# Three mixers: the last output product runs its last three weight units, not two, one half of the tokens at a time

## The chip, the cores and the metric

The kernel runs on one core of one Trainium2 chip. The metric is the device time of one execution in microseconds (us). TensorE (PE) multiplies matrices into PSUM, VectorE (DVE), ScalarE (ACT) and GpSimd (POOL) do the rest, SyncE (SP) issues the weight loads. Each engine takes its own list of instructions in order and waits on counters (semaphores) that the others raise.

## The reference, cut to what matters

Two blocks run over 256 tokens of width 1024, in eight sublayers in all, numbered s = 0 to 7. Sublayers 0, 3 and 6 are the three mixers (sparse attention with a convolution, differential attention, a gated recurrence); the others are SwiGLUs. Each mixer ends in a product of its 256x1024 result with a 1024x1024 output weight, and then a gated residual and a norm lead to the next sublayer's input:

```
# s = 0
mixed = jnp.concatenate([attn, conv_out], axis=-1)
mix = mixed @ w_out
x = layer_norm(DEEPNORM_ALPHA * x + g1[:, None, :] * mix, ln1_g[l], ln1_b[l])
ff = swiglu(modulate(x, sh2, sc2), w_gate[l], w_up[l], w_down[l])
...
# s = 3 and s = 6
y = diff_attention(...)      # ends in   o.reshape(B, S, H * dv) @ w_o
y = hgrn2(...)               # ends in   o.reshape(B, S, D_MODEL) @ w_o
x = x + gate[:, :, 1] * y
h = rms_norm(x, norm_g[layer, 2]) * (1.0 + scale[:, :, 2]) + shift[:, :, 2]
x = x + 0.5 * gate[:, :, 2] * swiglu_2(h, ffn_w_in[layer, 1], ffn_w_down[layer, 1])
```

## The kernel before

**Weights.** All large weights stream through a ring of three slots, in units of 128x2048 numbers (1 MB). SP loads a unit into `raw`; ACT copies its high part to `whi` (function `hi`, line 534), DVE takes the rest to `wlo` (function `lo`, line 910), and PE multiplies. A product of full precision is three matmuls: high times high, high times rest, rest times high (`three`, line 1523). A unit has a number; `w_used` counts the units that PE is done with, and `hi(unit)` waits until PE is done with the unit three places earlier, whose slot it takes. ACT executes whatever comes behind that `hi` only afterwards.

**Tokens.** The 256 tokens are two halves t = 0, 1 of 128. The output weight of a mixer is four units, here called u0 to u3. `rows_of` multiplies one unit with one token half: two halves h of the 1024 output columns, two slices of the contraction, three matmuls each, 12 matmuls of 512 columns. `down_rows` does that for both token halves of a unit and raises `w_used`. The sum over the four units grows in PSUM, banks 0 and 1 for t = 0, banks 2 and 3 for t = 1.

**The end of a sublayer.** `close` does the last two units by token half: t = 0 of both, then t = 1 of both. So the result of t = 0 is complete while PE still has work on t = 1. Between them PE does `sum_columns` (line 1633, 32 records: the next sublayer's shift and scale columns) and `transpose_inputs(s + 1, 0)` (line 1622, eight transposes of the new t = 0 input). For s = 0 both come after all four pieces.

**What answers to it on the other engines**, for s = 3 and 6. DVE (`conclude`): the residual of t = 0 (lines 966 and 971, halves h), `lo` of the next sublayer's first unit F (F takes the slot of u1), the new columns (lines 932, 937), `modulate` of t = 0 (line 944), the residual of t = 1 with the rest parts of the new input (line 952). ACT: `hi` of u3, `hi(F)`, then `leave`: two squares of t = 0 (line 565), the scaled copy of t = 0 (line 572) once POOL has taken the root (lines 462, 465), `modulate` (line 541), high parts (line 546), the first square of t = 1, `hi(F + 1)`, the second square, the scaled copy of t = 1. For s = 0 there are no squares on ACT: DVE sums the moments itself (lines 966, 977, 978), and the layer norm follows (lines 987, 989).

**The next sublayer** starts with `enter`: 12 matmuls of t = 0, the eight transposes of t = 1, and so on. In s = 0 DVE also adds up pieces of a large weight for the shift and scale columns (line 925), which arrive by DMA.

The order of each engine's list is written out by hand; nothing reorders it.

Of the kernel before, what the change touches and what calls it, by code (L numbers as in the profile page):

```python
# [30 lines left out]
P = 128  # L31
# [10 lines left out]
NSUB = 8  # L42
# [40 lines left out]
LATE_GATES = (1, 4, 7)  # L83
# [61 lines left out]
def two_blocks(  # L145
# [29 lines left out]
    with ExitStack() as ctx:  # L175
# [15 lines left out]
        hhi = sb("hhi", [P, KT, TOK], F32R)  # L191
        hlo = sb("hlo", [P, KT, TOK], F32R)
# [48 lines left out]
        def bank(b, n=1):  # L241
            return psf[:, b * BANK:(b + n) * BANK]
# [3 lines left out]
        w_hi, w_lo, w_used = sem("w_hi"), sem("w_lo"), sem("w_used")  # L246
# [7 lines left out]
        y_ready, x_new, root = sem("y_ready"), sem("x_new"), sem("root")  # L254
# [1263 lines left out]
        def _(pe):  # L1518
# [57 lines left out]
                                     g == 0 and k == 0 and ct % 2 == 0, g == 1 and k == 3, weights_move=False)  # L1576
                done.then_inc(w_used, 1)

            def rows_of(unit, hi_of, lo_of, t, first, final, lap=0, signal=None):

                slot = unit % RING
                if t == 0:
                    pe.wait_ge(w_lo, unit + 1 + RING * lap)
                for h in range(2):
                    for k in range(2):
                        cols = slice(k * D + h * BANK, k * D + (h + 1) * BANK)
                        done = three(bank(2 * t + h), hi_of(k, t), lo_of(k, t), whi[:, slot, cols], wlo[:, slot, cols],
                                     first and k == 0, final and k == 1)
                    if signal and h == 0:
                        done.then_inc(signal, 1)  # L1590
                return done

            def down_rows(unit, hi_of, lo_of, first, lap=0, before=None):

                for t in range(NT):
                    if before:
                        before(t)
                    done = rows_of(unit, hi_of, lo_of, t, first, False, lap)
                done.then_inc(w_used, 1)

            def close(s, one, two, before_one, before_two):

                before_one(0)
                rows_of(*one, 0, False, False)
                before_two()
                rows_of(*two, 0, False, True, signal=y_ready).then_inc(y_ready, 1)
                if 0 < s < NSUB - 1:
                    sum_columns(s + 1)
                before_one(1)
                rows_of(*one, 1, False, False).then_inc(w_used, 1)  # L1610
                if 1 < s < NSUB - 1:
                    transpose_inputs(s + 1, 0)
                rows_of(*two, 1, False, True, signal=y_ready).then_inc(w_used, 1)
                if s == 0:
                    sum_columns(1)
                if s < 2:
                    transpose_inputs(s + 1, 0)
# [19 lines left out]
            def sum_gate(s):  # L1637

                pe.wait_ge(a_used, pieces_until(s, 2) if s else KT)
                for h in range(2):  # L1640
                    done = pe.matmul(bank(gate_bank(s) + h), ones[:, :], ada_acc[:, s % 2, 2 * D + h * BANK:2 * D + (h + 1) * BANK],
                                     start=True, stop=True)
                done.then_inc(gate_sum, 1)

            def transpose_inputs(s, t):

                src = xs if s < 2 else xn
                for g in range(2):
                    if s == 0:
                        pe.wait_ge(x_land, 32)  # L1650
                        pe.wait_ge(vec_set, 1)
                    elif s == 1:
                        pe.wait_ge(x_new, 2 * t + g + 1)
                    else:
                        pe.wait_ge(h_src, 4 * (s - 2) + 2 * t + g + 1)
                    transposes([src[:, t, (4 * g + k) * P:(4 * g + k + 1) * P] for k in range(4)], 2 * t + g, h_tr)

            def output_product(s, unit, mixed_ready, k0=0):

                def place(j):  # L1660
                    k_j = (k0 + 2 * j) % KT
                    return (unit + j, lambda k, t: hhi[:, k_j + k, t * P:(t + 1) * P],
                            lambda k, t: hlo[:, k_j + k, t * P:(t + 1) * P])

                def mixed(j, t):
                    if (j, t) in mixed_ready:
                        pe.wait_ge(mix_lo, mixed_ready[j, t])

                for j in range(2):
                    down_rows(*place(j), j == 0, before=lambda t: mixed(j, t))  # L1670
                close(s, place(2), place(3), lambda t: mixed(2, t), lambda: None)

            def swiglu(s):
                m, turned = SWIGLUS.index(s) * NCH, SWIGLUS.index(s) * (NCH + 1)
                U = FIRST[s]

                def gate_up(unit, g, i, lap=0):

                    for t in range(NT):
                        if g == 0:  # L1680
                            pe.wait_ge(act_ready, 2 * (m + i) - 1 + t)
                        done = columns_of(unit, g, t, 4 + t, lap=lap)
                        if g == 1 and t == 0:
                            done.then_inc(gu_ready, 1)
                    done.then_inc(w_used, 1)

                def turn(i):
                    pe.wait_ge(act_ready, 2 * (m + i + 1))
                    pe.wait_ge(alo_ready, turned + i)
                    for k in range(2):  # L1690
                        for t in range(NT):
                            done = pe.transpose(ps[:, 6, k * TOK + t * P:k * TOK + (t + 1) * P],  # L1692
                                                act[:, t, k * P:(k + 1) * P], ident)
                    done.then_inc(tr_ready, 1)

                def last_turn(t):
                    pe.wait_ge(act_ready, 2 * (m + NCH - 1) + t + 1)
                    pe.wait_ge(alo_ready, turned + NCH - 1 + t)
                    for k in range(2):
                        done = pe.transpose(ps[:, 6, k * TOK + t * P:k * TOK + (t + 1) * P],  # L1700
                                            act[:, t, k * P:(k + 1) * P], ident)
                    done.then_inc(tr_ready, 1)

                def kept(unit):
                    return unit, lambda k, t: ahi[:, k, t * P:(t + 1) * P], lambda k, t: alo[:, k, t * P:(t + 1) * P]

                def body(first, i, lap=0, first_down=False):
                    gate_up(first, 0, i, lap)
                    if first_down and s not in LATE_GATES:
                        pe.wait_ge(gate_set, s + 1)  # L1710
                    turn(i - 1)
                    gate_up(first + 1, 1, i, lap)
                    pe.wait_ge(alo_ready, turned + i)
                    down_rows(*kept(first + 2), first_down, lap=lap)

                enter(s, (4, 5), gu_ready)
                body(U + 2, 1, first_down=True)
                if s == 1:

                    pe.wait_ge(toe_fill, 2)  # L1720
                    pe.wait_ge(cols_set, 2)
                    for h in range(HEADS):
                        if h >= 2:
                            pe.wait_ge(toe_rows, h - 1)
                        pe.matmul(ps[:, 6 + h % 2, 0:TOE], big[0:BUCKETS + 1, 2560 + h * P:2560 + (h + 1) * P],
                                  big[0:BUCKETS + 1, 2048:2048 + TOE], start=True, stop=True).then_inc(toe_mm, 1)
                    pe.wait_ge(toe_rows, HEADS)
                with pe.Fori(2, NCH - 1) as i:
                    body(U + 5, i, i - 2)
                last = U + 3 * (NCH - 1) - 1  # L1730
                gate_up(last, 0, NCH - 1)
                turn(NCH - 2)
                gate_up(last + 1, 1, NCH - 1)
                last_turn(0)

                def before_last():
                    last_turn(1)
                    if s in LATE_GATES:
                        sum_gate(s)

                def before_last_but_one(t):
                    if t == 1:
                        pe.wait_ge(alo_ready, turned + NCH + 1)

                close(s, kept(last + 2), (last + 3, lambda k, t: hhi[:, k, t * P:(t + 1) * P],
                                          lambda k, t: hlo[:, k, t * P:(t + 1) * P]), before_last_but_one, before_last)

            def attention():

# [286 lines left out]
```

## Time and profile before

| | |
|---|---|
| median of 3 runs | 1611.03 us (1610.11 to 1612.12) |
| the profiled execution's own time | 1611.54 us |
| its span, first to last instruction | 1609.5 us |
| PE busy | 1439.1 us, 89% |
| DVE, ACT, POOL busy | 68%, 42%, 12% |
| mean granted TensorE clock | 0.927 of 2.4 GHz |
| chain that ended last, on PE | 72% |

The profile counts an engine as busy while its compute instructions run. In a row of the timeline, the bracket at the end is how long the engine stood idle before and which instruction released it. The chain of waits is followed back from the last instruction, so its pieces show what each moment of the time was spent on. PEclk is the granted TensorE clock: 1.00 is 2.4 GHz and 0.50 is 1.2 GHz.

### The profile page before, as it was taken

The page shows a single profiled execution, that of the slowest core. Times are in us where ns is not written, and L with a number is a line of the kernel's source. Part 1 is how long each engine was busy: PE and PEld are TensorE (multiplying, and loading weights), DVE is VectorE, ACT ScalarE, POOL GpSimd, SP SyncE. Part 2 cuts the span into 40 slices and gives each one's busy share as a digit, 9 for nine tenths or more (in the row PEclk, how much of TensorE's full clock was granted, in tenths as well). Part 3 has the DMA queues.
Part 4 walks back from the last instruction along what each step waited for, and adds up shares of the span by engine and source line. Part 5 has one row for each costly group of instructions (what it writes and reads, how often), then busy time and mean ns, then how long its engine had stood idle before and what let it go on. Part 6 is the DMA issues. An engine that isn't in the chain of part 4 may idle for free.

```text
span 1609.5 us, 19253 instructions
## 1 busy us (share of the span) xinstructions
PE 1439.1 (89%) x6855; PEld 1193.9 (74%) x6855; DVE 1095.0 (68%) x1103; ACT 673.6 (42%) x788; POOL 193.8 (12%) x271
## 2 busy tenths in 40 slices
PE   1786769999889999996899999999999896899999
PEld 1785557888668888773678888788888785778887
DVE  4678674777657886657557775688865796455554
ACT  0433124444343443545364434544446752254432
POOL 1101230111031110210011110211101000100000
PEclk9887769999989999996799999999999997799999
DMA  7751726999558996450168895699944440146662
GB/s 298 255 184 29 247 73 204 311 317 325 179 195 290 352 335 211 147 193 0 54 220 297 306 312 168 221 320 337 348 157 158 154 134 26 53 152 220 210 224 80
DMA packets 183812, 333.97 MB, mean 208 GB/s; under 512 B 8666, under 2 KB 122943, under 8 KB 182610
## 3 DMA queue, kind: packets, MB, share of 16 engines
q1 hardware_dynamic: 157328, 237.95, 44.0%
q0 software_dynamic: 26112, 95.07, 16.6%
q8 instruction: 33, 0.54, 0.1%
q10 hardware_dynamic: 322, 0.27, 0.1%
q14 instruction: 17, 0.14, 0.0%
HBM read 330.64 MB, written 2.62 MB: 207 GB/s over the span
## 4 chain that ended last, share of the span: by engine, by line
PE 72%; DVE 15%; ACT 5%; DMA 3%; issue 2%; POOL 2%; ACTq 0%; POOLq 0%; DVEq 0%
PE ps L1523 65%; DVE wlo L910 2%; DMA ada_raw<-in_w_ada 2%; PE ps L1633 2%; PE ps L1622 1%; PE ps L1692 1%; DVE ada_acc L1464 1%; ACT whi L534 1%; ACT hf L541 1%; DMA raw<-in_w_ada 1%; DVE xn L966 1%; DVE ada_acc L925 1%; POOL st L462 1%; DVE ada_acc L1084 1%; DVE hlo L952 1%
## 5 line engine op out<-in xcount | busy, mean ns | idle before, releaser
L910 DVE TENSOR_TENSOR wlo<-raw,whi 128x2048 fp32r<-128x2048 f32 x215 | 490.4, 2285 | 164.7 <-ACT whi L534 164.3
L1523 PE MATMUL ps<-whi,hhi 128*128 128x512 f32 (+1 forms) x1208 | 490.2, 406 | 36.6 <-DVE hlo L952 16.0
L534 ACT ACTIVATE whi<-raw 128x2048 fp32r<-128x2048 f32 x215 | 410.0, 1910 | 244.4 <-PE ps L1523 217.7
L1523 PE MATMUL ps<-wlo,hhi 128*128 128x512 f32 (+1 forms) x1208 | 479.4, 397 | 0.0
L1523 PE MATMUL ps<-whi,hlo 128*128 128x512 f32 (+1 forms) x1208 | 479.1, 397 | 0.0
L1523 PEld LDWEIGHTS ps<-whi,hhi 128*128 128x128 f32 x1208 | 232.7, 193 | 92.9 <-DVE wlo L910 18.1
L1523 PEld LDWEIGHTS ps<-whi,hlo 128*128 128x128 f32 x1208 | 232.3, 192 | 50.3
L1523 PEld LDWEIGHTS ps<-wlo,hhi 128*128 128x128 f32 x1208 | 233.0, 193 | 46.5 <-issue 0.7
L925 DVE SCALAR_TENSOR_TENSOR ada_acc<-ada_raw,csil,ada_acc 128x1024 f32<-128x1024 f32 x120 | 150.3, 1278 | 13.1 <-DMA ada_raw<-in_w_ada 11.1
L1523 PE MATMUL ps<-whi,ahi 128*128 128x512 f32 x400 | 158.6, 396 | 0.0
L1523 PE MATMUL ps<-whi,alo 128*128 128x512 f32 x400 | 157.6, 394 | 0.0
L1523 PE MATMUL ps<-wlo,ahi 128*128 128x512 f32 x400 | 157.6, 394 | 0.0
L441 POOL DMA_DIRECT2D ada_raw<-in_ada_w x96 | 50.9, 530 | 542.4 <-DVE ada_acc L925 538.4
L610 ACT ACTIVATE ahi<-ps 128x512 fp32r<-128x512 f32 x50 | 29.9, 599 | 189.9 <-PE ps L1692 189.9
L606 ACT ACTIVATE act<-ps 128x256 f32<-128x256 f32 x110 | 42.2, 384 | 152.7 <-PE ps L1523 152.7
L1040 DVE TENSOR_TENSOR alo<-ps,ahi 128x512 fp32r<-128x512 f32 x50 | 34.5, 691 | 94.4 <-ACT ahi L610 94.4
L1523 PEld LDWEIGHTS ps<-whi,alo 128*128 128x128 f32 x400 | 76.2, 191 | 16.2
L1523 PEld LDWEIGHTS ps<-wlo,ahi 128*128 128x128 f32 x400 | 76.3, 191 | 15.8
L1523 PEld LDWEIGHTS ps<-whi,ahi 128*128 128x128 f32 x400 | 76.4, 191 | 15.7
L1523 PE MATMUL ps<-hhi,whi 128*128 128x256 f32 x224 | 67.1, 300 | 11.7 <-DVE wlo L910 11.7
L1523 PE MATMUL ps<-hhi,wlo 128*128 128x256 f32 x224 | 66.2, 296 | 0.0
L1523 PE MATMUL ps<-hlo,whi 128*128 128x256 f32 x224 | 66.0, 295 | 0.0
(237 smaller groups left out, 1389.9 us busy)
## 6 DMA issues: line engine op xcount, KB each, us to landing
raw<-in_ffn_w_in SPq DMA_DIRECT2D x176, 512.0 KB
ada_raw<-in_ada_w POOLq DMA_DIRECT2D x96, 512.0 KB, 5.2
raw<-in_ffn_w_down SPq DMA_DIRECT2D x44, 1024.0 KB
big<-in_ada_w POOLq DMA_DIRECT2D x48, 512.0 KB, 6.1
ada_raw<-in_w_ada POOLq DMA_DIRECT2D x32, 512.0 KB, 4.8
raw<-in_hgrn_w_in SPq DMA_DIRECT2D x16, 1024.0 KB
raw<-in_attn_w_qkv SPq DMA_DIRECT2D x12, 1024.0 KB
raw<-in_w_gate SPq DMA_DIRECT2D x22, 512.0 KB
```

Source lines behind the costliest of these rows:

```text
L441: pool.dma_start(ada_slot(p), w[bass.ds(kt * P, P), first + j * D:first + (j + 1) * D])\
L462: pool.tensor_scalar(mean, mean, st[:, 251 + 2 * t:252 + 2 * t], EPS2, ALU.add, ALU.add).then_inc(root_in, 1)
L534: sc.activation(whi[:, slot, 0:n], raw[:, slot, 0:n], ACT.Copy).then_inc(w_hi, 1)
L541: done = sc.activation(hf[:, kt, t * P:(t + 1) * P], ps[:, 2 * t + 1, k * P:(k + 1) * P], ACT.Identity, scale=modc[:, s % 2, 8 + kt:9 + kt ...
L606: sc.activation(act[:, t, :], ps[:, 4 + t, 0:FC], ACT.Silu).then_inc(silu_done, 1)
L610: sc.activation(ahi.rearrange("p k n -> p (k n)"), bank(6), ACT.Copy).then_inc(ahi_ready, 1)
L910: ve.tensor_tensor(wlo[:, slot, 0:n], raw[:, slot, 0:n], whi[:, slot, 0:n].bitcast(F32), ALU.subtract)\
L925: ve.scalar_tensor_tensor(acc, ada_slot(p), csil[:, bass.ds((0 if a < 2 else 8) + kt, 1)], acc, ALU.mult, ALU.add).then_inc(a_used, 1)
L952: ve.tensor_tensor(hlo[part], hf[part], hhi[part].bitcast(F32), ALU.subtract).then_inc(h_lo, 1)
L1040: ve.tensor_tensor(a_lo, bank(6), a_hi.bitcast(F32), ALU.subtract).then_inc(alo_ready, 1)
L1523: done = pe.matmul(dst, lhsT, rhs, start=first and n == 0, stop=final and n == 2, skip_group_check=True)
L1633: done = pe.matmul(ps[:, COL_BANK, j:j + 1], ada_acc[:, s % 2, j * P:(j + 1) * P], ones[:, 0:1], start=True, stop=True)
```

## The change

`close` takes a list of units in place of two. For the mixers the list has three, u1 to u3, and only u0 is done by `down_rows`; for the SwiGLUs it still has two, in the order as before. With three units the eight transposes of the next input stand between the two column halves (h = 0 and h = 1) of the last unit at t = 1, not ahead of that unit.

```
-            def rows_of(unit, hi_of, lo_of, t, first, final, lap=0, signal=None):
+            def rows_of(unit, hi_of, lo_of, t, first, final, lap=0, signal=None, between=None):
...
+                    if between and h == 0:
+                        between()
...
-            def close(s, one, two, before_one, before_two):
+            def close(s, places, before):
 
-                before_one(0)
-                rows_of(*one, 0, False, False)
-                before_two()
-                rows_of(*two, 0, False, True, signal=y_ready).then_inc(y_ready, 1)
+                last = len(places) - 1
+                for j, place in enumerate(places):
+                    before(j, 0)
+                    done = rows_of(*place, 0, False, j == last, signal=y_ready if j == last else None)
+                done.then_inc(y_ready, 1)
                 if 0 < s < NSUB - 1:
                     sum_columns(s + 1)
-                before_one(1)
-                rows_of(*one, 1, False, False).then_inc(w_used, 1)
-                if 1 < s < NSUB - 1:
-                    transpose_inputs(s + 1, 0)
-                rows_of(*two, 1, False, True, signal=y_ready).then_inc(w_used, 1)
+                for j, place in enumerate(places):
+                    turning = (lambda: transpose_inputs(s + 1, 0)) if j == last and 1 < s < NSUB - 1 else None
+                    if turning and last == 1:
+                        turning()
+                    before(j, 1)
+                    rows_of(*place, 1, False, j == last, signal=y_ready if j == last else None,
+                            between=turning if last > 1 else None).then_inc(w_used, 1)
...
-                for j in range(2):
-                    down_rows(*place(j), j == 0, before=lambda t: mixed(j, t))
-                close(s, place(2), place(3), lambda t: mixed(2, t), lambda: None)
+                down_rows(*place(0), True, before=lambda t: mixed(0, t))
+                close(s, [place(j) for j in range(1, 4)], lambda j, t: mixed(j + 1, t))
```

The first place is PE's list at the end of sublayer 3, from the matmuls on t = 0 to those on t = 1. A row that waits for `mix_lo` is the first matmul of u2 on a token half. Before, u2 at t = 0 comes behind all of u1, and after `sum_columns` (the rows on `ada_acc`) u2 follows at once:

```order
L1523 MATMUL ps<-whi,hhi 128x512 [waits w_lo,mix_lo]
L1523 MATMUL ps<-wlo,hhi 128x512
...
L1633 MATMUL ps<-ones,ada_acc 128x1 [waits cols_set,a_used]
L1633 MATMUL ps<-ones,ada_acc 128x1 x15
L1523 MATMUL ps<-whi,hhi 128x512 [waits mix_lo]
L1523 MATMUL ps<-wlo,hhi 128x512
```

Now:

```order
L1638 MATMUL ps<-ones,ada_acc 128x1 [waits cols_set,a_used]
L1638 MATMUL ps<-ones,ada_acc 128x1 x15
L1523 MATMUL ps<-whi,hhi 128x512
L1523 MATMUL ps<-wlo,hhi 128x512
L1523 MATMUL ps<-whi,hlo 128x512
...
L1523 MATMUL ps<-whi,hhi 128x512 [waits mix_lo]
```

The 12 matmuls of u1 on t = 1 moved from ahead of u2 and u3 at t = 0 to behind `sum_columns`. `w_used` for u1 is raised by the last of them, so its place moved too.

The second place is PE's list a little later: the eight transposes of sublayer 4's first token half (the rows on `xn`) and what follows them. Before, 12 matmuls of u3 lie behind them, of which the last three are shown, ahead of the first matmul of sublayer 4 (the row that waits for `h_lo`):

```order
L1622 MATMUL ps<-kc,xn 128x128 [waits h_src]
L1622 MATMUL ps<-kc,xn 128x128 x3
...
L1523 MATMUL ps<-whi,hhi 128x512
L1523 MATMUL ps<-wlo,hhi 128x512
L1523 MATMUL ps<-whi,hlo 128x512
L1523 MATMUL ps<-whi,hhi 128x512 [waits h_lo,w_lo]
```

Now six matmuls lie between, all shown:

```order
L1627 MATMUL ps<-kc,xn 128x128 [waits h_src]
L1627 MATMUL ps<-kc,xn 128x128 x3
L1523 MATMUL ps<-whi,hhi 128x512
L1523 MATMUL ps<-wlo,hhi 128x512
L1523 MATMUL ps<-whi,hlo 128x512
L1523 MATMUL ps<-whi,hhi 128x512
L1523 MATMUL ps<-wlo,hhi 128x512
L1523 MATMUL ps<-whi,hlo 128x512
L1523 MATMUL ps<-whi,hhi 128x512 [waits h_lo,w_lo]
```

The transposes moved behind six more matmuls. The lists of ACT, DVE, POOL and SP are the same before and after. ACT's at this place, where the three rows on `whi` are `hi` of u2, u3 and F:

```order
L534 ACTIVATE whi<-raw 128x2048 [waits w_used,w_land0]
L534 ACTIVATE whi<-raw 128x2048 [waits w_used,w_land1]
L534 ACTIVATE whi<-raw 128x2048 [waits w_used,w_land2]
L565 ACTIVATE xn,st<-xs 128x512 [waits x_new] x2
L572 ACTIVATE xn<-xs,st 128x512 [waits root]
```

Nothing moved there; the two squares and the scaled copy stand behind the `hi` of F, as before.

## Rows read from the trace of the kernel before

**Rows 1.** The page, busy time (share of the span) xinstructions.
```profile
PE 1439.1 (89%) x6855; PEld 1193.9 (74%) x6855; DVE 1095.0 (68%) x1103; ACT 673.6 (42%) x788; POOL 193.8 (12%) x271
```

**Rows 2.** What TensorE waited for, 776 to 832 us: us, times, longest.
```profile
PE ps L1622 <- DVE big L1353: 4.8, 1, 4.8
PE ps L1622 <- ACT xn L572: 2.8, 1, 2.8
PE ps L1523 <- DVE hlo L952: 0.8, 1, 0.8
```

**Rows 3.** Chain of waits, end of sublayer 3: start us, us, what.
```profile
799.46 3.47 PE ps L1633 x32
802.93 2.89 PE ps L1523 x12
...
806.69 1.40 PE ps L1523 x6
```

**Rows 4.** Timeline of ACT, end of sublayer 3: start us, us.
```profile
794.12 1.92 ACT L534 ACTIVATE whi<-raw 128x2048 fp32r<-128x2048 f32 x1 [3.52 <-PE ps L1523]
799.66 0.63 ACT L565 ACTIVATE xn<-xs 128x512 f32<-128x512 f32 x1 [3.63 <-DVE xs L971]
...
800.99 0.63 ACT L565 ACTIVATE xn<-xs 128x512 f32<-128x512 f32 x1 [0.60 <-DVE xs L971]
...
804.01 1.34 ACT L572 ACTIVATE xn<-xs,st 128x512 f32<-128x512 f32 x2 [2.29 <-POOL st L465]
806.79 1.50 ACT L541 ACTIVATE hf<-ps,modc 128x128 f32<-128x128 f32 x4 [1.44 <-PE ps L1622]
...
810.19 1.90 ACT L534 ACTIVATE whi<-raw 128x2048 fp32r<-128x2048 f32 x1
812.00 0.61 ACT L565 ACTIVATE xn<-xs 128x512 f32<-128x512 f32 x1
```

**Rows 5.** Timeline of DVE, the same stretch.
```profile
798.21 0.69 DVE L966 TENSOR_TENSOR xn<-ps,gate 128x512 f32<-128x512 f32 x1 [5.29 <-PE ps L1523]
...
800.87 2.29 DVE L910 TENSOR_TENSOR wlo<-raw,whi 128x2048 fp32r<-128x2048 f32 x1
...
810.77 0.69 DVE L971 TENSOR_TENSOR xs<-xs,xn 128x512 f32<-128x512 f32 x1
```

**Rows 6.** Chain of waits, end of sublayer 6.
```profile
1399.28 4.08 PE ps L1633 x32
1403.36 5.33 PE ps L1523 x12
1408.69 0.97 PE ps L1622 x8
...
1419.03 1.97 PE ps L1622 x8
```

**Rows 7.** Windows of 2 us: PE, PEld, DVE, ACT, POOL busy (count), PEclk, DMA share, GB/s.
```profile
816.00:818.00 2.00, 1.95 (x12) 1.63 (x13) 1.26 (x4) 1.25 (x3) 1.85 (x1) 1.00 0.89 348
1420.00:1422.00 2.00, 2.00 (x8) 1.78 (x7) 1.37 (x4) 0.97 (x3) 0.61 (x1) 0.50 1.11 387
```

**Rows 8.** Timeline, end of sublayer 0.
```profile
193.43 0.65 PE L1523 MATMUL ps<-whi,hhi 128*128 128x512 f32 x1 [4.74 <-DVE wlo L910]
...
204.91 0.68 DVE L966 TENSOR_TENSOR xn<-ps,gate 128x512 f32<-128x512 f32 x1
205.05 4.99 PE L1633 MATMUL ps<-ones,ada_acc 128*128 128x1 f32 x32 [1.56 <-DVE ada_acc L925]
...
213.96 1.11 PE L1622 MATMUL ps<-kc,xs 128*128 128x128 f32 x4 [3.92 <-DVE xs L989]
```

**Rows 9.** Chain of waits, start of sublayer 1.
```profile
226.67 4.62 PE ps L1523 x12
...
235.19 14.07 PE ps L1523 x48
...
249.69 10.91 PE ps L1523 x48
```

More of the change, by code:

```diff
@@ L1734, in swiglu, with before @@
                 last_turn(0)
[L1736 to L1742, printed above, removed]
+                def before(j, t):
+                    if (j, t) == (1, 0):
+                        last_turn(1)
+                        if s in LATE_GATES:
+                            sum_gate(s)
+                    elif (j, t) == (0, 1):
                         pe.wait_ge(alo_ready, turned + NCH + 1)
-                close(s, kept(last + 2), (last + 3, lambda k, t: hhi[:, k, t * P:(t + 1) * P],
-                                          lambda k, t: hlo[:, k, t * P:(t + 1) * P]), before_last_but_one, before_last)
+                close(s, [kept(last + 2), (last + 3, lambda k, t: hhi[:, k, t * P:(t + 1) * P],
+                                           lambda k, t: hlo[:, k, t * P:(t + 1) * P])], before)
             def attention():
```

## The prediction, made before the changed kernel ran

> **What bounds the kernel now.** I read the page first: PE is busy for 89% of the span [rows 1], and most of the chain of waits is PE. Inside the SwiGLUs PE hardly pauses, so the change can only act at the three places where a mixer hands over to a SwiGLU. There I read what PE waited for, then the chain, then the timeline of ACT and DVE. At the end of sublayer 3 PE loses 4.8 us ahead of the output product, which the change doesn't touch, then 0.8 us for the rest part of the new input and 2.8 us for the scaled copy of t = 1 [rows 2]. The eight transposes of t = 0 don't appear among the waits: the scaled copy runs from 804.01 to 805.35 [rows 4], and the last matmul piece ahead of them ends at 802.93 + 2.89 = 805.82 [rows 3]. Their cover is just enough, with 0.5 us to spare. So the change lengthens a cover that was not short. The end of sublayer 6 has the same pattern, about 3 us stretched by a slower clock.
>
> **Part 1: t = 0 is ready earlier.** 12 matmuls of u1 leave the stretch ahead of the result of t = 0. At full clock 48 matmuls take 10.91 us [rows 9], so 12 take 2.73 us; `sum_columns` starts that much earlier, at 796.7 and not 799.46 [rows 3]. DVE's first residual could start at 795.5 and not 798.21 [rows 5]. u3 at t = 0 then starts near 794.0, and still finds its rest part: `lo` of u3 ends before that by about 1 us, as DVE waits 5.29 us between it and the residual at 798.21 [rows 5] (it ended at 792.9).
>
> **Part 2: u1 is released later, and ACT stands behind it.** This is the step on which I rest the forecast. `hi` of F waits until PE is done with u1. Before, that was at 794.1: the row at 794.12 is it, released by PE [rows 4]. Then ACT was idle for 3.63 us until DVE delivered the residual [rows 4], so the copy cost nothing. Now u1 ends behind `sum_columns`: 796.7 + 3.47 + 2.89 [rows 3] = 803.1. ACT's next instructions are the two squares and the scaled copy of t = 0, and they stand behind that copy. From there, with durations of [rows 4]: copy 1.92, to 805.0; first square with its read-out 0.73 (less than the 1.33 between the two starts, which was DVE's pace), to 805.7; from the start of the second square to the scaled copy 804.01 - 800.99 = 3.02, to 808.75; half of the scaled copy's 1.34, 0.7, to 809.5. The first four transposes go at 809.5, the other four at 810.15 with the second half, done at 810.65. PE had reached them at 803.1 + 2.73 + 1.40 [rows 3] = 807.2, so it idles 2.3 us where it did not wait before. ACT's `modulate` of t = 0 follows at about 810.8, where it was at 806.79 [rows 4]: 4.0 us late.
>
> What follows hangs on that `modulate`: the high and rest parts of t = 0, then ACT's square of t = 1, `hi(F + 1)`, the second square, the root, the scaled copy of t = 1 and its transposes. Of the six matmuls left of u3 (1.40 us [rows 3]) PE is done at 812.1, and it waits 2 us for the rest part, where it waited 0.8 us; the wait of 2.8 us stays as it is [rows 2]. Check by idle time: 2.3 + 2.0 + 2.8 = 7.1 us against 3.6, or 3.5 more, against a delay of 4.0 by the chain, whose remainder is the split transposes. Taken: **4.0 us in sublayer 3**, and nothing of it comes back, since all that is behind hangs on PE.
>
> The same for sublayer 6: `sum_columns` from 1399.28 - 2.73 = 1396.55, then 4.08 and, at half clock, 5.33 for 12 matmuls [rows 6], to 1405.95; then the same 1.92 + 0.73 + 3.02 + 0.7, to 1412.3, with the durations of [rows 4]. Before, the transposes of t = 0 were at 1408.69 [rows 6] by the chain, 1408.5 by start. Late by 3.8 us, and 3.9 with the split transposes. If the fall of the clock there doesn't come, u1 is done 2.5 us earlier, and only 1.4 us are lost.
>
> **What else waits behind these.** On DVE `lo` of F (before at 800.87 [rows 5]) now waits for the copy, to 805.0, and ends at 807.3, ahead of the transposes at 809.5. So it hides; behind it stand only the new columns, for which nobody waits earlier. SP's loads behind `lo` of F are issued some 4 us later, but so is PE's demand for them. POOL only takes the roots. The DMA queues are otherwise untouched.
>
> That ACT doesn't run a ready square past a waiting or running copy, the trace shows: DVE had finished the second residual of t = 1 at 810.77 + 0.69 = 811.46 [rows 5], and the square began at 812.00, when the copy of 810.19 [rows 4] was over.
>
> The Trainium skill's page "TensorE: Matmul & The Clock Gate" (section "Architectural detail: the array is 16× 32×32, not 1× 128×128") says it as a rule: ScalarE and VectorE are strict FIFO, and only TensorE pulls weight loads ahead. By this rule the two sites cost 7.9 us; were it not so, they would cost what the first rival says. The trace agrees, by the 0.54 us above.
>
> **Part 3: sublayer 0.** Here ACT has no squares, and nothing hangs on its `hi(F)` until DVE's `lo(F)`, which stands behind the moments. PE waits for the rest part of u3 until 193.43 [rows 8]. Now it comes there 2.7 us earlier and waits longer; behind it stand 48 matmuls and not 36, so it ends 2.7 us later, at about 206.2, and `sum_columns` follows at once, where it waited 1.56 us until 205.05 [rows 8]. With 4.99 us it ends at 211.2. The transposes wait for DVE's layer norm until 213.96 [rows 8], and DVE starts that chain at 204.91, behind the last piece of the shift and scale sums, with the result of t = 0 long there. So 1.2 us later on PE is covered by the idle 3.92 us, and I take **0**. Bounds: if the clock stayed high through this handover, 12 matmuls would take 2.73 and not 4.62 us, and 48 would take 10.91 and not 14.07 [rows 9], at most 5 us gained, of which the first 1.9 can give under 1 as the transposes behind wait for DVE; upward 1 us.
>
> **Part 4: the clock.** The handover has more idle time now. At sublayer 3 the clock stayed at 1.00 when PE came back at 816, at sublayer 6 it was at 0.50 in the same place [rows 7], and from the second transposes to the same row of the SwiGLU sublayer 6 took 1.0 us longer (1.97 us for the eight transposes alone [rows 6]). With the idle time doubled I expect sublayer 3 to lose this too: **1.0 us**, bounds 0 and 3.4, the latter if it also falls at `sum_columns` as in sublayer 6 (12 matmuls in 5.33 and not 2.89).
>
> **Sum.** 4.0 + 3.9 + 0 + 1.0 = 8.9 us on the profiled execution's own 1611.54, so 1620.4. That execution lies 0.5 us above the median of 1611.03; on the median it is 1619.9, and I say **1620.0 us**.
>
> **Rivals.**
> - *ACT's copy doesn't hold the squares* (u1 is released in time for some reason that I mis-stepped). Then the scaled copy of t = 0 is ready 2.7 us earlier than before, but the transposes stand six matmuls later: 803.1 + 2.73 + 1.40 = 807.2 against 805.8, 1.4 us late at both sites. Time: 1611.0 + 2.8 = 1613.8. For it: ACT was idle on both sides of that copy before. Against: the place of `w_used` for u1 in PE's list.
> - *The earlier result carries through, on the other side.* If the chain that decides begins with the result of t = 0 and nothing else holds it, each of the two handovers ends 2.7 us earlier: 1611.0 - 5.5 = 1605.5. It decides from the point where PE waits for the transposes of t = 0 with the work ahead of them as it was; the 0.5 us to spare [rows 3, 4] is how far the trace is from that. Against it: PE didn't wait for the transposes of t = 0 before, so an earlier result has no wait to shorten.
> - *The clock is kind in sublayer 6*: no fall at `sum_columns`. There 1.4 us and not 3.9 are lost: 1617.5. For it: of the two sites sublayer 3 has no fall [rows 3]. Against: in sublayer 6 `sum_columns` and what lies ahead of it keep their lengths, so the fall has the same cause as before [rows 6].
> - *The clock falls at both `sum_columns`*: 2.4 us more in sublayer 3: 1622.4.
>
> **Chances.** Forecast 0.52, kind clock 0.15, both fall 0.17, no hold 0.09, earlier result 0.05, something else 0.02. A change of less than 0.2% (3.2 us) can't be told from none here. The forecast and both clock cases lie beyond it on the slow side, the first rival inside, the second beyond it on the fast side. Faster 0.05, within 0.2% 0.09, slower 0.86. The range reaches down to the first rival's neighbourhood and up past the case with both falls: 1614.5 to 1624.0.
>
> **What would show it.** In the changed profile, at both handovers ACT's copy of F stands behind `sum_columns` (near 803 and 1406), released by PE; the squares follow it without a gap; PE shows a new wait of about 2.3 us for the scaled copy (line 572) ahead of the first transposes, and a wait of 2 us for the rest part; the SwiGLUs start 4 us late each. Sublayer 0 hands over at the same time as before. I am wrong if the squares run before the copy, if the new wait is under 1 us, or if sublayer 1 starts more than 1 us away from before.

## The result, and the profile after

The changed kernel took 1616.96 us (median of 7 runs, 1613.48 to 1618.88) where the kernel before took 1610.11 (7 runs, 1607.79 to 1612.12): 6.9 us slower between the medians; the ratio is 1.0044, 95% interval 1.0032 to 1.0056, which is 7.1 us. The profiled execution took 1617.90 us with a span of 1615.8 us, against 1611.54 and 1609.5. Timed again on another occasion (e4 below) the ratio was 1.0039 (1.0026 to 1.0053). Where a difference below is said to be by the ratio, it is the ratio's distance from 1 times the time before; for some runs it differs from that of the medians by 1 us and more.

The chain of waits of the changed kernel at the end of sublayer 3 (start us, us, what):

```profile
780.81 15.17 PE ps L1523 x60
795.98 3.46 PE ps L1638 x32
799.45 4.30 PE ps L1523 x12
...
803.83 1.92 ACT whi L534
805.74 1.24 ACT xn L565 x4
...
807.07 1.17 POOL st L462
...
808.32 0.58 POOL st L465
...
808.92 0.73 ACT xn L572
...
809.69 1.28 PE ps L1627 x8
...
811.06 1.51 ACT hf L541 x4
```

`sum_columns` (now line 1638) comes behind 60 matmuls, 15.17 us after the product's first one; before it came behind 72:

```profile
781.73 17.73 PE ps L1523 x72
```

The last 12 matmuls ahead of ACT's copy are u1 on t = 1. Then the chain leaves PE: copy, two squares, root, scaled copy, transposes, where before it ran through PE alone. ACT's own rows:

```profile
787.92 1.92 ACT L534 ACTIVATE whi<-raw 128x2048 fp32r<-128x2048 f32 x1 [2.77 <-PE ps L1523]
803.83 1.92 ACT L534 ACTIVATE whi<-raw 128x2048 fp32r<-128x2048 f32 x1 [13.99 <-PE ps L1523]
805.65 0.61 ACT L565 ACTIVATE xn<-xs 128x512 f32<-128x512 f32 x1
...
806.26 0.62 ACT L565 ACTIVATE xn<-xs 128x512 f32<-128x512 f32 x1
...
808.92 1.33 ACT L572 ACTIVATE xn<-xs,st 128x512 f32<-128x512 f32 x2 [1.95 <-POOL st L465]
```

ACT stood idle for 13.99 us until PE was done with u1, and the squares follow its copy with no gap; before, the copy had run at 794.12 and the squares waited for DVE [rows 4]. What PE waited for between 778 and 836 us (us, times, longest), to be held against [rows 2]:

```profile
PE ps L1627 <- ACT xn L572: 4.7, 2, 3.1
PE ps L1627 <- DVE big L1353: 4.6, 1, 4.6
PE ps L1523 <- DVE hlo L952: 1.6, 1, 1.6
```

The scaled copy is waited for twice, not once: 1.6 us ahead of the first transposes besides 3.1 us ahead of the second. (The wait of 4.6 us stands ahead of the output product, as before.) At the end of sublayer 6 the chain has the same shape, but with PE at full clock through `sum_columns` and u1:

```profile
1402.87 3.46 PE ps L1638 x32
1406.34 2.90 PE ps L1523 x12
...
1409.32 1.92 ACT whi L534
...
1415.19 1.28 PE ps L1627 x8
...
1425.47 1.97 PE ps L1627 x8
```

Here the 12 matmuls took 2.90 us where the 12 behind `sum_columns` took 5.33 before [rows 6]. To compare executions whose starts differ, the table takes the distance from the first matmul of a mixer's output product to the eight transposes of t = 1, and from there to the same matmul of the SwiGLU (its loop's start, 831.85 us in the profile of before), all from the traces:

| kernel | sublayer 3: to second transposes | on to the SwiGLU's loop | sublayer 6: to second transposes | on to the loop | time against before (95% interval) |
|---|---|---|---|---|---|
| before | 34.3 | 15.8 | 38.2 | 16.8 | |
| before, again (e10) | 34.3 | 15.8 | 38.3 | 16.9 | 1.0005 (0.9989 to 1.0021) |
| changed | 39.2 | 17.0 | 38.3 | 16.7 | 1.0044 (1.0032 to 1.0056) |
| changed, again (e4) | 39.1 | 17.0 | 38.3 | 16.7 | 1.0039 (1.0026 to 1.0053) |
| e1, sublayer 0 alone | 34.4 | 15.8 | 38.3 | 16.8 | 0.9991 (0.9978 to 1.0003) |
| e2, sublayer 3 alone | 39.4 | 17.0 | 38.5 | 16.9 | 1.0018 (1.0005 to 1.0032) |
| e3, sublayer 6 alone | 34.4 | 15.8 | 38.5 | 16.8 | 1.0006 (0.9995 to 1.0018) |
| e5, copy moved on ACT | 37.0 | 16.7 | 39.4 | 15.8 | 1.0020 (1.0003 to 1.0038) |
| e6, transposes not split | 40.5 | 16.8 | 43.4 | 15.8 | 1.0073 (1.0048 to 1.0098) |
| e7, both | 36.8 | 16.8 | 39.2 | 15.8 | 1.0021 (1.0007 to 1.0035) |
| e8, old order, copy held | 42.0 | 17.0 | 46.3 | 15.8 | 1.0105 (1.0078 to 1.0133) |
| e9, sum_columns later | 35.5 | 17.0 | 39.2 | 15.8 | 1.0019 (1.0005 to 1.0033) |
| e11, late copy of F + 1 | 36.7 | 16.2 | 36.8 | 16.2 | 0.9982 (0.9967 to 0.9997) |
| e12, early transposes | 34.9 | 17.7 | 37.0 | 16.1 | 0.9954 (0.9938 to 0.9969) |

So sublayer 3 costs 4.8 + 1.2 = 6.1 us (before rounding), sublayer 6 nothing.

### The profile page after: what moved, and what is told of

It is laid out like the page before. It is cut to its first block, busy times and chain, and to the rows that moved or that the text cites. A ratio compares the mean times of both kernels' runs of the same rounds, so it can differ in the third digit from the quotient of the medians.

```text
span 1615.8 us, 19253 instructions
## 1 busy us (share of the span) xinstructions
PE 1448.6 (90%) x6855; PEld 1201.2 (74%) x6855; DVE 1094.8 (68%) x1103; ACT 673.2 (42%) x788; POOL 193.1 (12%) x271
## 4 chain that ended last, share of the span: by engine, by line
PE 72%; DVE 15%; ACT 5%; DMA 3%; issue 2%; POOL 2%; ACTq 0%; POOLq 0%; DVEq 0%
PE ps L1523 65%; DVE wlo L910 2%; DMA ada_raw<-in_w_ada 2%; PE ps L1638 2%; PE ps L1627 1%; PE ps L1696 1%; ACT whi L534 1%; DVE ada_acc L1464 1%; ACT hf L541 1%; DVE ada_acc L1084 1%; POOL st L462 1%; DVE ada_acc L925 1%; ACT xn L565 1%; PE ps L1791 1%; PE ps L1729 1%
```

## The experiments

Each was timed against the kernel before in the same session.

**e1, e2, e3: one mixer at a time.**

```
-                down_rows(*place(0), True, before=lambda t: mixed(0, t))
-                close(s, [place(j) for j in range(1, 4)], lambda j, t: mixed(j + 1, t))
+                kept_back = 1 if s in (0,) else 2        # (3,) in e2, (6,) in e3
+                for j in range(kept_back):
+                    down_rows(*place(j), j == 0, before=lambda t: mixed(j, t))
+                close(s, [place(j) for j in range(kept_back, 4)], lambda j, t: mixed(j + kept_back, t))
```

> Three units by token half in sublayer 0 only; sublayers 3 and 6 as before. Theory 'ACT's copy holds the squares': sublayer 0 has no squares, so nothing on the path moves; time equal to before within 1 us, unless the clock at the start of sublayer 1 changes (the 48 matmuls after the second transposes took 14.07 us before and 11.22 us with the change), then up to 2.9 us faster. Rival 'PE's extra wait for u3 counts': u3's rest part is waited for 2.7 us longer, so 2.7 us slower.

> Three units by token half in sublayer 3 only. Theory 'ACT's copy holds the squares': from the first matmul of the product to the second transposes 39.2 us if the clock falls at sum_columns as in the full change, 37.9 if not (before: 34.3), so 4 to 5 us slower in all. Rival 'the split transposes cost it': 1.4 us slower.

> Three units by token half in sublayer 6 only. Theory: the copy holds the squares here too, but the result depends on the clock at sum_columns: from the product's first matmul to the second transposes 38.3 us without a fall (equal to before, 38.2, which had one) and 40.7 us with one; so 0 to 2.5 us slower. Rival 'something in the full change gave the time back ahead of sublayer 6': 4 us slower alone.

e1: 1610.85 us, no change that can be told. PE's wait for u3's rest part grew, as its row shows (timeline of PE in e1), to 6.64 us from 4.74 [rows 8], and cost nothing:

```profile
196.23 0.79 PE L1523 MATMUL ps<-whi,hhi 128*128 128x512 f32 x1 [6.64 <-DVE wlo L910]
```

So the rival for sublayer 0 falls. e2: 39.4 us at its site, as expected with a fall of the clock, and 1.0018 in time. e3: 38.5 us at its site with no fall at `sum_columns`, and 1.0006. In sum the three ratios give 1.0015 where the whole change has 1.0039 to 1.0044; with intervals of about 0.0013 on each side these don't exclude each other, but they don't show that the parts add up either. e2's profile shows 5.0 + 1.2 us at its site; its timed runs 2.9 us by the ratio (0.8 to 5.2), 4.1 us between the medians.

**e4, e10: both kernels once more,** unedited, for the spread of profiles.

> The changed kernel once more, on the same chip as the partial ones. Expected 6 to 7 us slower than before. If the clock's falls at sum_columns are a matter of the single execution, this profile has them at other places than the first profile of the same kernel, and the piece times of PE differ there by 2 us and more; if they belong to the kernel, the same places show again.

> The kernel before, once more with its profile. Theory 'the 2.6 us that the changed kernel was ahead at the start of sublayer 2 are the clock of one execution': this profile differs from the first one of the same kernel by 1 to 4 us between sublayer 0's product and sublayer 2, with the clock's falls there at other places; at the ends of sublayers 3 and 6 the falls are where they were (none at 3, one at sum_columns of 6).

Both sites repeat to 0.2 us. Elsewhere one and the same kernel differs. The stretch from the loop of sublayer 5 to the second transposes of sublayer 6's input took 180.8 us in the first profile of before and 182.3 in the second. Its chain of waits around `sum_columns`, first profile, then second:

```profile
1192.73 3.46 PE ps L1633 x32
1196.20 4.45 PE ps L1523 x12
1200.65 0.89 PE ps L1622 x8
```

```profile
1193.82 3.94 PE ps L1633 x32
1197.76 5.33 PE ps L1523 x12
1203.09 1.12 PE ps L1622 x8
```

The work is the same and the clock isn't: in the first profile PEclk is back at 0.86 in the window from 1200 to 1202 us, in the second it is still 0.50 there. The span of before was 1612.4 us this time, 2.9 us above the first. A single span can't carry a statement of 2 us about this kernel.

The expectation of e10 names another such place, and the profiles do differ there. From the second transposes of sublayer 1's input to that sublayer's loop the first profile of before took 18.7 us, the second 17.5, the changed kernel 15.7 and then 17.5, and e11, whose list there is that of before, 15.6. So the 2.6 us by which the changed kernel's first profile was ahead at that loop come without the change too.

**e5: the hold taken away on ACT.** Of the changed kernel:

```
                 hi(U + 15)
-                hi(FIRST[4])        # and hi(FIRST[7]) in sublayer 6
...
                     scaled(s, 0)
+                if s in (3, 6):
+                    hi(FIRST[n])
```

> The changed kernel with ACT's high part of F moved behind the scaled copy of t = 0 in sublayers 3 and 6, so that the squares no longer wait for u1. Theory 'ACT's copy holds the squares': PE has no wait for the scaled copy ahead of the first transposes, product start to second transposes at sublayer 3 shrinks from 39.2 to 34.3 + 1.4 = 35.7 us (plus up to 2.4 if the clock falls), and the kernel gains 3 us or more on the changed one. Rival 'the split transposes cost it': no gain, within 1 us of the changed kernel.

ACT's timeline in e5 has the first square 15.3 us behind the product's first matmul, where the changed kernel has 24.8, and the copy of F behind the squares:

```profile
794.21 0.63 ACT L565 ACTIVATE xn<-xs 128x512 f32<-128x512 f32 x1 [6.34 <-DVE xs L971]
...
797.34 1.34 ACT L572 ACTIVATE xn<-xs,st 128x512 f32<-128x512 f32 x2 [1.08 <-POOL st L465]
801.88 1.92 ACT L534 ACTIVATE whi<-raw 128x2048 fp32r<-128x2048 f32 x1 [3.20 <-PE ps L1523]
```

What PE waited for in e5, 776 to 838 us:

```profile
PE ps L1627 <- DVE big L1353: 4.7, 1, 4.7
PE ps L1627 <- ACT xn L572: 2.9, 1, 2.9
PE ps L1523 <- DVE hlo L952: 1.7, 1, 1.7
```

One wait for the scaled copy is left, the old one. The second transposes come 2.2 us sooner than in the changed kernel, and the time falls from 1.0039 to 1.0020 above before; the gain on e4 is 3.1 us by the ratios, though the two intervals overlap. What is left of the loss at sublayer 3 (37.0 against 34.3) is about the 1.4 us by which the first transposes stand later in PE's list, and up to 1.8 us of clock: 30 matmuls behind `sum_columns` took 8.58 us where 10.91 us for 48 [rows 9] makes 6.8.

**e9: the hold shortened on PE,** with ACT's list as in the changed kernel: `sum_columns` no longer stands ahead of u1, so u1 is released sooner.

```
-                if 0 < s < NSUB - 1:
+                if 0 < s < NSUB - 1 and last == 1:
                     sum_columns(s + 1)
...
                             between=turning if last > 1 else None).then_inc(w_used, 1)
+                    if j == 0 and last > 1 and 0 < s < NSUB - 1:
+                        sum_columns(s + 1)
```

> The changed kernel with sum_columns in sublayers 3 and 6 moved behind u1 at t = 1, so that u1 is released 3.5 us earlier. ACT's list is untouched. Theory 'ACT's copy holds the squares': the copy of F starts near 799.6 by the changed kernel's clock (3.5 us earlier than 803.8), the wait of 2.5 us ahead of the first transposes goes, and the time falls to that of the version with the copy moved on ACT, about 3 us below the changed kernel. Rival 'the order of the units or the split costs it': the time of the changed kernel.

1.0019, the same as e5 by another way. ACT's squares still stand behind the copy of F, but the copy starts 18.0 us behind the product's first matmul, not 23.0, and the scaled copy is begun at 803.74, before PE gets to the transposes. The chain of waits of e9 at the end of sublayer 3 stays on PE up to the first transposes, at full clock:

```profile
780.70 17.86 PE ps L1523 x72
798.55 3.46 PE ps L1640 x32
802.02 4.25 PE ps L1523 x18
806.27 0.89 PE ps L1629 x8
...
816.15 1.27 PE ps L1629 x8
```

The second transposes stand at 816.15 - 780.70 = 35.5 us, 1.1 above before. The prediction's first rival, the world without the hold, had 1.4. Of the 3.7 us by which this is below the changed kernel 1.4 are clock, since the 12 matmuls of u1 took 4.30 us there.

**e6, e7: the transposes ahead of the whole last unit,** in the changed kernel and in e5.

```
-                    if turning and last == 1:
+                    if turning:
                         turning()
...
-                            between=turning if last > 1 else None).then_inc(w_used, 1)
+                            ).then_inc(w_used, 1)
```

> The changed kernel with the eight transposes of t = 0 ahead of the whole last unit, as before the change, and the hold left in. Theory 'hold': the transposes start when the scaled copy is there, as in the changed kernel, so PE's wait grows from 2.5 to about 3.9 us and 12 matmuls in place of 6 stand behind them: the rest part is then waited for 1.4 us less. The time of the changed kernel, within 1 us. Rival 'split': 2.8 us faster than the changed kernel.

> Both: no hold and the transposes of t = 0 ahead of the whole last unit. Only the order of the units differs from before. Both theories: PE reaches the transposes at the same moment as before (all work ahead of them is the same), with the scaled copy ready 2.7 us earlier; product start to second transposes 34.3 us at sublayer 3, the time of before within 1 us.

e6 is slower than the changed kernel, 1.0073 (6 runs), where I had written the same time within 1 us. In its profile the residual of t = 1 starts later at sublayer 3, and ACT's first square of t = 1, which followed the high parts without a gap in the changed kernel, now waits for DVE (ACT's timeline in e6):

```profile
810.80 1.16 ACT L546 ACTIVATE hhi<-hf 128x512 fp32r<-128x512 f32 x2
813.18 0.63 ACT L565 ACTIVATE xn<-xs 128x512 f32<-128x512 f32 x1 [1.23 <-DVE xs L971]
```

That alone doesn't refute the expectation, for the excess is mostly clock. Behind the first transposes e6 had PEclk at 0.50 from 810 to 812 us, the changed kernel 1.00. From the first transposes to the second e6 took 11.6 us, where the same list took 10.4 in the kernel before; with 10.4 the second transposes would stand at 39.3, against 39.2 in the changed kernel. At sublayer 6 the first transposes came 3.3 us later than in the changed kernel, and there `sum_columns` and u1 took 4.67 + 4.88 us and not 3.46 + 2.90. Whether the wait, which the edit lengthened (2.93 us against 1.64), brought the falls isn't shown.

e7 has neither hold nor split: 1.0021. The expectation for the site, the time of before within 1 us, was missed at sublayer 3, with 36.8 against 34.3 us. The chain of waits shows a second hold, on DVE:

```profile
797.96 4.35 PE ps L1523 x12
...
802.39 1.93 ACT whi L534
...
804.34 2.29 DVE wlo L910
...
806.94 1.37 DVE hf L944 x4
808.31 0.60 DVE xn L966
```

`lo` of F waits for the copy of F, the copy waits for u1, and behind `lo` of F stand the new columns, `modulate` of t = 0 and the residual of t = 1 in DVE's list. In the kernel before that `lo` was over at 803.16 [rows 5]. The 12 matmuls at the head of this chain took 4.35 us and not 2.89 [rows 3], so 1.5 of the 2.4 us are clock and about 1.0 the second hold. At sublayer 6, where the clock falls before as in e7, the chain takes the same way, and the second transposes are 1.0 us late too; a higher clock behind them gives it back (the two stretches sum to 55.0 us, and 55.1 before).

**e8: the hold alone, on the old order.**

```
                 hi(U + 15)
+                sc.wait_ge(w_used, used(U + 14))      # U + 18 in sublayer 6
                 hi(FIRST[4])
```

> The kernel before, in its old order of units, with ACT's copy of F in sublayers 3 and 6 made to wait until PE is done with u2 on both token halves (805.6 us in the profile of before at sublayer 3, where u1 was done at 794.1). Theory 'hold': the squares start at 807.5, so the first transposes at 805.7 + 1.9 + 0.7 + 2.7 + 0.7 = 811.7, 6.0 us late at each of two sites, 12 us slower in all, less 2 where the clock doesn't fall. Rival 'split or order of units': no change.

1626.48 us, 1.0105: 17 us slower by the ratio (15.5 between the medians), with PE's list untouched. ACT's copy started 803.72 - 779.53 = 24.2 us behind the product's first matmul, and the first transposes stand at 30.1 against 23.9 before, 6.1 late; expected were 6.0. The chain of waits of PE in e8:

```profile
797.33 3.46 PE ps L1635 x32
800.79 2.90 PE ps L1525 x12
...
809.58 1.97 PE ps L1624 x8
```

At sublayer 6 they are 6.1 us late too. The second transposes are 7.7 us late at sublayer 3 and 8.1 at sublayer 6, more than the 12 us expected in all. What is above 6.1 is clock: behind the wait of 5.9 us PEclk is 0.50, and at sublayer 3 the first eight transposes took 1.97 us and the six matmuls behind them 2.02, against 0.87 and 1.40 before, with the same list.

**e11: a hold of the same kind, found in the kernel before.** In `leave`, the copy of F + 1 stands between the two squares of t = 1 [rows 4, at 810.19].

```
                 if s > 1:
                     square(s, 1, 0)
+                    square(s, 1, 1)
                 hi(FIRST[n] + 1)
                 if s == 1:
                     square(s, 1, 0)
-                if s:
                     square(s, 1, 1)
+                if s:
```

> The kernel before with one edit on ACT: in sublayers 2 to 6 the high part of F + 1 stands behind the second square of t = 1, not ahead of it. The square starts when DVE's residual is there (811.5 and not 812.0 at sublayer 3), the copy runs beside POOL's root. 0.5 us earlier at each of five handovers: 2.5 us faster than before if the clock is the same; the rest part of F + 1 is 1.4 us later, which PE doesn't reach earlier.

1609.57 us, 0.9982: 2.9 us faster by the ratio (0.5 to 5.3), 2.4 between the medians; 2.5 were expected. The number fits by luck, for the mechanism was larger than I had it. At sublayer 6 the second transposes come 1.4 us sooner, not 0.5, and the two stretches sum to 53.0 against 55.0 us; at sublayer 3 they come later, since this profile has a fall of the clock there. Besides the 0.5 us, POOL's first step of the root got shorter. Before and then e11, at sublayer 6:

```profile
1415.78 1.78 POOL L462 TENSOR_SCALAR st<-st 128x1 f32<-128x1 f32 x1 [11.99 <-ACT xn L565]
```

```profile
1414.11 0.30 POOL L462 TENSOR_SCALAR st<-st 128x1 f32<-128x1 f32 x1 [11.49 <-ACT xn L565]
```

Before, DVE's `lo` of F + 1 (line 910, 2.29 us) ran at that time, from 1415.11 to 1417.40, and POOL's step ended 0.17 us behind it; in e11 `lo` starts only at 1415.85. Against that, "which PE doesn't reach earlier" failed: the chain of e11 now passes through this `lo` into the SwiGLU's matmuls, and PE waits 0.4 us for it.

**e12: three units without the hold.** e5 and e11 together, with the transposes ahead of u2 on t = 1 and, on DVE, the columns and `modulate` of t = 0 ahead of `lo(F)`.

```
-                    turning = (lambda: transpose_inputs(s + 1, 0)) if j == last and 1 < s < NSUB - 1 else None
-                    if turning and last == 1:
+                    turning = (lambda: transpose_inputs(s + 1, 0)) if j == 1 and 1 < s < NSUB - 1 else None
+                    if turning:
                         turning()
...
                     residual(s, 0, 1)
-                    lo(FIRST[n])
+                    if s not in (3, 6):
+                        lo(FIRST[n])
                 set_columns(n)
                 ve.wait_ge(cols_set, n + 1)
                 modulate(n, 0)
+                if s in (3, 6):
+                    lo(FIRST[n])
```

> Three units by token half as in the change, without the hold (ACT's high part of F behind the scaled copy), with the transposes of t = 0 behind u1 at t = 1, DVE's modulate of t = 0 ahead of the rest part of F, and the edit of the late copy. Theory: the input of t = 0 is complete while PE still works on u2 and u3, so the wait for the rest part (0.8 us) goes and the second transposes start about 1 us earlier at sublayers 3 and 6; with 0.5 us at three other handovers 3 us faster than before, up to 7 us faster without falls of the clock, and equal to before where the clock falls at sublayer 3 as in the other three-unit versions.

1605.77 us, 0.9954 (0.9938 to 0.9969): 7.4 us faster than before by the ratio, 6.2 between the medians, and below both kernels. What PE waited for, 776 to 838 us:

```profile
PE ps L1631 <- DVE big L1357: 4.4, 1, 4.4
PE ps L1631 <- ACT xn L572: 1.4, 1, 1.4
PE ps L1527 <- DVE hlo L953: 0.8, 1, 0.8
PE ps L1527 <- DVE wlo L911: 0.4, 1, 0.4
```

The wait for the scaled copy is 1.4 us where it was 2.8 [rows 2], as in e11, which has the same edit. The wait for the rest part, 0.8 us, was to go and stayed, and the second transposes came sooner at sublayer 6 alone (37.0 against 38.2), where e11 had 36.8. Of the 7.4 us some 3 are e11's edit. The other 3.8 us between the medians of e11 and e12 are not explained: in the profiles the two handovers of e12 take 52.6 and 53.1 us and those of e11 52.9 and 53.0, with falls of the clock in both. That the order of three units gives them is possible and not shown; the edit of DVE's list and the new place of the transposes came with it, and no run has these alone.

## Why the prediction was right

Forecast slower by 8.9 us, to 1620.0; measured 7.1 us slower by the ratio, 1616.96, inside 1614.5 to 1624.0. The mechanism was right, two sizes were not, and the time lies nearer to the rival with the kind clock (1617.5) than to the forecast.

- **Part 1** (t = 0 ready earlier): 2.73 us forecast for `sum_columns`, 2.56 measured.
- **Part 2, the hold.** Forecast: copy of F behind `sum_columns`, released by PE, squares with no gap. So it was. e8 makes such a loss with nothing but this hold, and e5, which removes it, and e9, which shortens it, win back some 3 us each. The term of sublayer 3 was 4.0 us; the transposes came 4.8 us late. The difference is clock: the 12 matmuls behind `sum_columns` took 4.30 us, not 2.89. Against that the way from the second square to the scaled copy took 2.66 us, not 3.02. This way holds POOL's root, whose first step took 1.17 us (before 1.51) and takes 0.30 when DVE's `lo` isn't running (see the last section). So `lo` of F probably didn't hide, as I had written that it would: by these durations it added 0.9 us to the root.
- **Part 2, sublayer 6: the step that was mis-sized.** I wrote "then 4.08 and, at half clock, 5.33 for 12 matmuls" and took 3.9 us. They took 3.46 and 2.90, since the clock didn't fall at `sum_columns`, in both profiles of the changed kernel and in e3. The hold is there (the chain above), but the second transposes are at 38.3 against 38.2 us. I had this as a rival, with 1.4 us left over where 0.1 was measured, and had given it 0.15. At the first transposes 0.3 us were left over: the 1.4 left out that `sum_columns` too is shorter without the fall (3.46 and not 4.08 us), and the way to the scaled copy was shorter by 0.4 us, as at sublayer 3. That the range still held the time is in part luck: a term of 3.9 us came out at nothing, and no other was as wrong.
- **The waits.** Forecast 2.3 us ahead of the first transposes and 2.0 for the rest part; measured 1.6 and 1.6, as slower matmuls filled part of the first.
- **Part 3** (sublayer 0 costs nothing): e1, 0.9991. PE's first transposes there came 0.4 us later than before, counted from the start.
- **Part 4** (clock, 1.0 us at sublayer 3 behind the second transposes): 15.8 became 17.0. The fall at `sum_columns` was in the upper bound and came too.
- **By the traces** the sites give 6.1 us of the 6.3 between the two spans. Elsewhere the changed profile was 2.6 us ahead at the start of sublayer 1's loop, of which 0.9 was left at the first matmul of sublayer 3's product; it lost 1.6 us on the way into sublayer 6 and gained 0.3 within it. e10 shows that such differences come without any change.
- **The rivals.** "ACT's copy doesn't hold the squares" and "the earlier result carries through" fell with the first chain. Whether the earlier result carries through once the copy, the transposes and `lo(F)` are placed for it, as in e12, is open: the kernel is faster, but its handovers don't show it.

Open is where the clock falls. At `sum_columns` of sublayer 3 it does in six of the seven versions with three units there (not in e9) and in neither profile of before; at sublayer 6 it does in both profiles of before and in e5, e6, e7, e9 and e12, but not in the changed kernel or e3. e11, in the old order, fell at sublayer 3 too, so it isn't the order of the units alone.

## What to carry to other kernels

When work is reordered on one engine, follow each counter that it raises to every engine that waits for it, and ask what stands behind that wait in the other engine's list: here a copy that nobody needed yet held two squares on which the next sublayer hung. When one such hold is taken away, look for the next: e7 had none on ACT and one on DVE. An earlier result is worth something only if a wait existed for it and the queues of all engines between let it through; the same reorder lost 7 us with the queues as they were, and with the lists of PE, ACT and DVE rearranged around it the kernel was 7 us ahead of the old one (some 3 of them from e11's edit, the rest unexplained). And before a difference of 1 to 3 us is put down to an order of instructions, compare the granted clock in the same windows: it made most of the excess in e6 and of that above 6 us per site in e8.

## What was unexpected of the hardware

- The same kernel's profiles differ by 1.6 us in one handover (180.8 and 182.3 us, above) with nothing but the granted clock at another place. Over this stretch, which no edit touched, twelve profiles (all but e11's and e12's, where an edit touches it) fall into groups near 179.2, 180.8 and 182.3 us.
- The clock fell from 2.4 to 1.2 GHz during or just behind the 32 one-column records of `sum_columns` at several handovers (e10's second chain above is one), while PE was not idle at all. The 12 matmuls behind it then took up to 5.33 us, not 2.9. From the start of the first of them to the start of the last it was 2.64 us at 18 of the 84 places in all 14 profiles (ends of sublayers 1 to 6), and 3.6 to 4.8 us at 66.
- POOL's first step of the root (line 462, one column of 128 numbers) took 0.30 us or between 1.16 and 1.79, with the same operands. In the 14 profiles it appears 168 times. In 124 of them DVE's `lo` (line 910, or 911 and the like in other versions) was running when it began, and it ended 0.16 or 0.17 us behind that `lo`; in the other 44 it took 0.30 or 0.31. It reads as if one engine's instruction held another's, though `lo` raises no counter that this step waits for; the runs show the coincidence without an exception, and not its reason.
